# A decoder layer whose input is turned raw: root applied at read-out, merge gates scaled and put through tanh at the branch sums

## What is computed

```
h = x * rsqrt(mean(x^2) + 1e-6) * attn_norm
[MoBA q,k,v | NSA q, kv(cmp,slc,win) | NSA gates | merge gates] = h @ w_in
y_A = block-sparse attention (8 heads);  y_B = compressed, selected and window attention (8 heads, 2 kv groups)
x = x + (sigmoid(gA) * (y_A W_A) + sigmoid(gB) * (y_B W_B)) @ W_o
x = x + W_down(gelu(conv_a) * conv_b),  conv = causal conv3 of (RMSNorm(x) @ W_up)
x = x + sigmoid(x @ W_pg) * (p @ W_pp)
```

## Time and profile before

| | us |
|---|---|
| median of 3 runs | 888.48 |
| lowest, highest | 887.63, 891.33 |
| the profiled execution | 890.37 |
| its span, first to last instruction | 888.5 |
| busy PE, DVE, ACT, POOL | 863.6, 378.0, 405.8, 425.3 |

### The profile page before, as it was taken

How to read it: one execution, slowest core, us unless ns; L and a number is a source line. 1 busy time by engine, 2 the same in 40 slices (tenths; PEclk the granted TensorE clock), 3 DMA queues, 4 the chain that set the end, 5 groups by cost and what they waited for, 6 DMA issues and landing times.

```text
span 888.5 us, 13023 instructions
## 1 busy us (share of the span) xinstructions
PE 863.6 (97%) x4471; PEld 726.9 (82%) x4471; DVE 378.0 (43%) x864; ACT 405.8 (46%) x882; POOL 425.3 (48%) x547
## 2 busy tenths in 40 slices
PE   8999999999799999999999999999999999999998
PEld 8899889887688776788887888888888888888886
DVE  5446665555545534444417444444444440020223
ACT  5224656566646667533433744444444442231321
POOL 3841764554534345644552644444444444454440
PEclk9999999999999999999999999999999999999999
DMA  6944443342121226266531633333333333332214
GB/s 188 232 109 131 107 103 95 96 113 60 37 60 50 70 85 214 81 233 211 187 95 56 206 94 95 95 98 101 99 97 106 99 98 98 97 102 86 83 62 140
DMA packets 101363, 99.30 MB, mean 112 GB/s; under 512 B 15956, under 2 KB 76084, under 8 KB 101300
## 3 DMA queue, kind: packets, MB, share of 16 engines
q1 hardware_dynamic: 101247, 98.48, 37.7%
q10 hardware_dynamic: 53, 0.01, 0.0%
HBM read 87.58 MB, written 10.88 MB: 111 GB/s over the span
## 4 chain that ended last, share of the span: by engine, by line
PE 88%; DVE 4%; ACT 3%; issue 2%; POOL 2%; SPq 0%; DMA 0%; ACTq 0%; DVEq 0%; POOLq 0%
PE banks L1491 26%; PE banks L1492 25%; PE banks L1493 25%; PE banks L1672 3%; PE banks L1650 2%; PE banks L1630 1%; PE banks L1629 1%; PE banks L1551 1%; PE banks L1680 1%; ACT attention_split L875 1%; DVE plain_arena L1290 1%; DMA plain_arena<-in_conv_w_dram 0%; DVE plain_arena L1257 0%; PE banks L1579 0%; PE banks L1508 0%
## 5 line engine op out<-in xcount | busy, mean ns | idle before, releaser
L698 POOL TENSOR_TENSOR split_arena<-plain_arena,split_arena 128x512 fp32r<-128x512 f32 x184 | 240.2, 1318 | 252.0 <-ACT split_arena L932 232.5
L1491 PE MATMUL banks<-split_arena 128*128 128x512 f32 (+3 forms) x808 | 304.2, 376 | 5.3 <-ACT plain_arena L838 2.1
L1493 PE MATMUL banks<-split_arena 128*128 128x512 f32 (+3 forms) x808 | 296.8, 367 | 0.0
L1492 PE MATMUL banks<-split_arena 128*128 128x512 f32 (+3 forms) x808 | 296.7, 367 | 0.0
L932 ACT ACTIVATE split_arena<-plain_arena 128x512 fp32r<-128x512 f32 x184 | 112.9, 627 | 190.0 <-PE banks L1493 175.2
L1491 PEld LDWEIGHTS banks<-split_arena 128*128 128x128 f32 x808 | 152.4, 189 | 31.9 <-issue 3.5
L1493 PEld LDWEIGHTS banks<-split_arena 128*128 128x128 f32 x808 | 152.0, 188 | 21.1
L1492 PEld LDWEIGHTS banks<-split_arena 128*128 128x128 f32 x808 | 152.4, 189 | 20.3 <-issue 0.5
L1491 PE MATMUL banks<-late_arena,split_arena 128*128 128x512 f32 x240 | 93.8, 391 | 0.0
L1493 PE MATMUL banks<-late_arena,split_arena 128*128 128x512 f32 x240 | 93.5, 390 | 0.0
L1492 PE MATMUL banks<-late_arena,split_arena 128*128 128x512 f32 x240 | 93.5, 389 | 0.0
(11 more groups left out here) (193 smaller groups left out, 1113.4 us busy)
## 6 DMA issues: line engine op xcount, KB each, us to landing
plain_arena<-in_w_up_dram SPq DMA_DIRECT2D x88, 256.0 KB, 3.2
plain_arena<-in_w_down_dram SPq DMA_DIRECT2D x44, 256.0 KB, 2.6
plain_arena<-in_w_in_dram SPq DMA_DIRECT2D x18, 512.0 KB, 4.2
plain_arena<-in_w_in_dram SPq DMA_DIRECT2D x32, 192.0 KB, 4.0
plain_arena<-in_x_dram SPq DMA_DIRECT2D x8, 512.0 KB, 5.0
gates<-plain_arena SPq DMA_DIRECT2D x16, 256.0 KB, 2.4
plain_arena<-skew SPq DMA_DIRECT2D x16, 256.0 KB, 4.6
plain_arena<-gates SPq DMA_DIRECT2D x16, 256.0 KB, 3.6
```

Source lines behind the costliest of these rows:

```text
L698: pool.tensor_tensor(W2l[:, c % RING, :], raw2[:, c % RING, :], W2h[:, c % RING, :].bitcast(F32), ALU.subtract).then_inc(w2_lo, 1)
L1491: nc.tensor.matmul(o, ah, bh, start=first, stop=False)
L1492: nc.tensor.matmul(o, ah, bl, start=False, stop=False)
L1493: return nc.tensor.matmul(o, al, bh, start=False, stop=last)
```

## The change

x is turned as it comes, in two halves of 256 tokens; the squares and the root run beside it. `take_proj` multiplies each token tile by its root as it empties PSUM. Gates are kept and spilled raw; PE spreads the root over a 128 x 512 tile `rstd_row` (diagonal matrices times ones), and at the branch sums DVE multiplies each gate tile by it (`scale_gate_a`, `scale_gate_b`) and ACT applies the tanh (`tanh_gate_a`, `tanh_gate_b`). Gate b tiles get six places in memory (two used twice), and their loads move from chunks 15, 18 and 24 to 9, 13 and 15. Transfers are reordered: the gain first, x 0 and 1, the weights of unit 0, x 2 and 3, constants, then the rest. In unit 0 to 1, copies move from POOL to DVE, the high parts of unit 1 go to ACT and its low parts to DVE; POOL makes its table ahead of gate 0. In the steps, unit 3 is split one step earlier, unit 6 gets a second bank for one tile, and TILE and TURN of units 6 and 7 move (unit 6: TILE 35, 38, 39, 42, TURN 37, 40, 41, 44).

The diff, cut to its core (indentation of eight blanks taken off):

```diff
     row += count
-split0 = b0 - 8 if w == 7 else b0 - 7
+split0 = b0 - 8 if w in (3, 7) else b0 - 7
...
         late += 1
+    gap, lead = (3 if w == 6 else 2), (2 if w >= 6 else 1)
     for a in range(2):
-        TILE[t + 2 + late + 2 * a], TURN[t + 3 + late + 2 * a] = (w, 2 * half + a), (w, 2 * half + a)
+        TILE[t + 2 + late + gap * a], TURN[t + 2 + late + gap * a + lead] = (w, 2 * half + a), (w, 2 * half + a)
...
         eng.wait_ge(raw0_in[kt // 4], 32)
-        eng.wait_ge(x_sq, NT)
...
         return 7 * (tt % 2)
+    if w == 6:
+        return 7 * (tt == 1)
...
 def vec_bank(w, x):
-    return 4 if w <= 1 and x % 2 else 1
+    if w == 0:
+        return (1, 4, 3, 5)[x]
+    return 4 if w == 1 and x % 2 else 1
...
+def turned_part(half, kt):
...
+    wk = A["w_in"].rearrange("l (k p) n -> p (l k) n", p=P)
+    sp.dma_start(rows[0:8, 0, :], A["attn_norm"].rearrange("l (r c) -> (l r) c", c=P)).then_inc(gain_in, 16)
+    for half in range(2):
+        for tt in range(2 * half, 2 * half + 2):
+            sp.dma_start(xnat[:, tt, :], x_d[tt]).then_inc(x_in[tt], 16)
+        if half == 0:
+            for part in range(2):
+                ks = slice(4 * part, 4 * part + 4)
+                sp.dma_start(raw[:, ks, 0:256], wk[:, ks, C_KC:C_KC + 256]).then_inc(raw0_in[part], 16)
+                sp.dma_start(raw[:, ks, 256:280], wk[:, ks, C_NG:C_NG + 24]).then_inc(raw0_in[part], 16)
...
         sp.dma_start(w2c[:, v, :], A[nm].rearrange("l k n -> (l k) n")).then_inc(w2c_in, 16)
-    sp.wait_ge(x_turned, KT)
-    sp.dma_start(w1[0], w1_d[0]).then_inc(w1k_in, 16)
...
     sp.dma_start(w1[1], w1_d[1]).then_inc(w1k_in, 16)
+    sp.wait_ge(x_turned, 2 * KT)
+    sp.wait_ge(x_sq, NT)
+    sp.dma_start(w1[0], w1_d[0]).then_inc(w1k_in, 16)
...
     def load_gate_b(k):
-        if k >= 2:
-            sp.wait_ge(br_sum, k - 1)
-        sp.dma_start(gb[:, k % 2, :], gate_d[8 + k]).then_inc(gb_in[k % 2], 16)
+        if k >= 6:
+            sp.wait_ge(br_sum, k - 5)
+        elif k >= 2:
+            sp.wait_ge(pv_done, values_count[T - 1])
+        if k >= 4:
+            sp.wait_ge(gb_scaled, k // 2 * 2 - 2)
...
         load_chunk(c)
-        if c == 15:
+        if c == 9:
...
             load_gate_b(3)
+        if c == 13:
+            load_gate_b(4)
+            load_gate_b(5)
+        if c == 15:
+            load_gate_b(6)
+            load_gate_b(7)
...
             load_gates_a(1)
-            load_gate_b(4)
-            load_gate_b(5)
...
-        if c == 24:
-            load_gate_b(6)
-            load_gate_b(7)
...
-    split_gate(0)
...
     ins.then_inc(rtab_done, 1)
-    pool.wait_ge(cst_done, 1)
-    for tt in range(2):
-        pool.wait_ge(qkv_done, tt + 1)
-        for a in range(2):
-            ins = pool.tensor_copy(qn[:, tt, :, a * DH:(a + 1) * DH], qkv[:, tt, 0:256].rearrange("p (v c) -> p v c", v=4))
-    ins.then_inc(dup_pool, 1)
-    split_unit(1, range(KT))
+    split_gate(0)
+    pool.wait_ge(cst_done, 2)
...
             act.wait_ge(g_out, 16 * j)
-        nc.scalar.activation(gstage, PS[:, 7, :], ACT.Tanh, scale=0.5).then_inc(gate_tanh, 1)
+        nc.scalar.activation(gstage, PS[:, 7, :], ACT.Copy).then_inc(gate_taken, 1)
...
+    def h_high(half, kt):
+        act.wait_ge(x_turned, KT * half + kt // 2 * 2 + 2)
+        nc.scalar.activation(hTh[:, kt, 256 * half:256 * half + 256], turned_part(half, kt), ACT.Copy, scale=cst[:, kt:kt + 1]).then_inc(hT_hi, 1)
...
+    act.wait_ge(cst_turned, 1)
+    nc.scalar.activation(cst[:, 0:8], PS[:, 0, 0:8], ACT.Copy).then_inc(cst_done, 1)
+    square_x(0)
     act.wait_ge(cst_done, 1)
+    for kt in range(4):
+        h_high(0, kt)
+    for k in (0, 2):
+        w_high(0, range(k, k + 2))
+        h_high(0, k + 4)
+        h_high(0, k + 5)
+    w_high(0, range(4, KT))
+    square_x(2)
     for kt in range(KT):
-        act.wait_ge(x_turned, kt + 1)
-        nc.scalar.activation(hTh[:, kt, :], PS[:, turn_bank(kt), :], ACT.Copy, scale=cst[:, kt:kt + 1]).then_inc(hT_hi, 1)
+        h_high(1, kt)
+    w_high(1, range(KT))
+    act.wait_ge(cst_turned, 4)
+    nc.scalar.activation(cst[:, 8:CONVW + P + 4], PS[:, 2, 8:CONVW + P + 4], ACT.Copy).then_inc(cst_done, 1)
...
     nc.scalar.activation(gsig, qkv[:, :, 256:280], ACT.Tanh, scale=0.5).then_inc(gsig_tanh, 1)
+    act.wait_ge(rstd_spread, 1)
+    nc.scalar.activation(rstd_row, PS[:, 6, :], ACT.Copy).then_inc(rstd_row_done, 1)
...
+    def tanh_gate_a(i):
+        act.wait_ge(ga_scaled, i + 1)
+        nc.scalar.activation(ga[:, i % 4, :], ga[:, i % 4, :], ACT.Tanh, scale=0.5).then_inc(ga_tanh, 1)
...
+    def tanh_gate_b(i):
+        act.wait_ge(gb_scaled, i + 1)
+        nc.scalar.activation(gb[i], gb[i], ACT.Tanh, scale=0.5).then_inc(gb_tanh, 1)
...
+    for i in range(4):
+        tanh_gate_a(i)
...
         e = c - RING
+        if e == 2:
+            for i in range(4):
+                tanh_gate_b(i)
+        if e == 8:
+            tanh_gate_b(4)
+            tanh_gate_b(5)
+        if e == 12:
+            for i in range(4, 8):
+                tanh_gate_a(i)
+        if e == 13:
+            tanh_gate_b(6)
+            tanh_gate_b(7)
...
+    def square_x(tt):
+        dve.wait_ge(x_in[tt], 16)
+        nc.vector.tensor_tensor_reduce(out=square_out[:, tt, :], in0=xnat[:, tt, :], in1=xnat[:, tt, :], scale=1.0, scalar=0.0,
+                                       op0=ALU.mult, op1=ALU.add, accum_out=ssx[:, tt:tt + 1]).then_inc(x_sq, 1)
...
+    def h_low(half):
+        for kt in range(KT):
+            q = slice(256 * half, 256 * half + 256)
+            dve.wait_ge(hT_hi, KT * half + kt // 2 * 2 + 2)
+            nc.vector.scalar_tensor_tensor(out=hTl[:, kt, q], in0=turned_part(half, kt), scalar=cst[:, kt:kt + 1],
+                                           in1=hTh[:, kt, q].bitcast(F32), op0=ALU.mult, op1=ALU.subtract).then_inc(hT_lo, 1)
...
+    square_x(1)
+    dve.wait_ge(cst_done, 1)
+    h_low(0)
+    square_x(3)
+    h_low(1)
+    gate_high(0)
+    gate_low(0)
     dve.wait_ge(x_sq, NT)
+    rsqrt(rstd, ssx, 1.0 / D, 4)
     dve.wait_ge(pool_const, 4)
+    for tt in range(NT):
+        ins = nc.vector.tensor_scalar(rstd_diag[:, tt * P:(tt + 1) * P], ident, rstd[:, tt:tt + 1], None, ALU.mult)
+        if tt == 0:
+            ins.then_inc(rstd_done, 1)
+    ins.then_inc(rdiag_done, 1)
+    for tt in range(2):
+        dve.wait_ge(qkv_done, tt + 1)
+        for a in range(2):
+            ins = nc.vector.tensor_copy(qn[:, tt, :, a * DH:(a + 1) * DH], qkv[:, tt, 0:256].rearrange("p (v c) -> p v c", v=4))
+    ins.then_inc(dup_dve, 1)
...
+    def shift_tokens(x):
+        dve.wait_ge(tcmp_a, x + 1)
+        nc.vector.tensor_copy(tcmp[DH:P, x, 0:S - 1], PS[DH:P, vec_bank(0, x), 1:S]).then_inc(tcmp_b, 1)
...
+    for kt in range(4):
+        w_low_one(1, kt)
+    for x in range(2):
+        shift_tokens(x)
+    for kt in range(4, KT):
+        w_low_one(1, kt)
+    for x in range(2, 4):
+        shift_tokens(x)
+    dve.wait_ge(cst_done, 2)
...
         link(nc.vector.tensor_scalar(cst[:, c:c + 1], cst[:, c:c + 1], -(DH ** -0.5), None, ALU.mult))
-    gate_high(0)
-    gate_low(0)
-    split_unit(1, range(KT))
...
+    def scale_gate_a(i):
+        dve.wait_ge(ga_in, 64 * (i // 4 + 1))
+        nc.vector.tensor_tensor(ga[:, i % 4, :], ga[:, i % 4, :], rstd_row, ALU.mult).then_inc(ga_scaled, 1)
...
+    def scale_gate_b(i):
+        dve.wait_ge(gb_in[i // 2 % 2], 32 * (i // 4 + 1))
+        nc.vector.tensor_tensor(gb[i], gb[i], rstd_row, ALU.mult).then_inc(gb_scaled, 1)
...
+    dve.wait_ge(rstd_row_done, 1)
...
         for m in range(4):
+            scale_gate_a(4 * mg + m)
+        for m in range(4):
             dve.wait_ge(chunk_done, cidx[("bra", mg, 3)] + 1)
-            dve.wait_ge(ga_in[m], 16 * (mg + 1))
+            dve.wait_ge(ga_tanh, 4 * mg + m + 1)
...
                                            op0=ALU.add, op1=ALU.mult).then_inc(brA_done, 1)
+        for i in range(4) if mg == 0 else (6, 7):
+            scale_gate_b(i)
...
             dve.wait_ge(chunk_done, cidx[("brb", mg, 3)] + 1)
-            dve.wait_ge(gb_in[i % 2], 16 * (i // 2 + 1))
+            dve.wait_ge(gb_tanh, i + 1)
             dve.wait_ge(brA_done, i + 1)
-            nc.vector.scalar_tensor_tensor(out=gb[:, i % 2, :], in0=gb[:, i % 2, :], scalar=1.0, in1=PS[:, 4 + m, :],
+            nc.vector.scalar_tensor_tensor(out=gb[i], in0=gb[i], scalar=1.0, in1=PS[:, 4 + m, :],
...
             dve.wait_ge(brB_done, i + 1)
-            nc.vector.tensor_tensor(ga[:, m, :], ga[:, m, :], gb[:, i % 2, :], ALU.add).then_inc(br_sum, 1)
+            nc.vector.tensor_tensor(ga[:, m, :], ga[:, m, :], gb[i], ALU.add).then_inc(br_sum, 1)
...
                                            op0=ALU.mult, op1=ALU.subtract).then_inc(mT_lo, 1)
+        if mg == 0:
+            scale_gate_b(4)
+            scale_gate_b(5)
...
     def turn_consts():
-        pe.wait_ge(const_in, 16 * 11)
+        pe.wait_ge(const_in, 16 * 10)
```

(37 more changed lines are left out.)

137 lines of the change are left out of this document (59 added, 78 removed).

## The result

The changed kernel takes 896.66 us (median of 4 runs, 895.23 to 897.89) where the kernel before takes 888.06 beside it: a ratio of 1.0086, 95% interval 1.0068 to 1.0104. It is slower, by 8.6 us; the forecast was 8.1 us faster. Its profiled execution took 897.32 us, with a span of 895.5 against 888.5.

The account below looks back on a forecast made before the run. PE, busy 863.6 of 888.5 us, was taken as the bound, so only its stands and slow-clock stretches could pay. Gains of 13.5 less losses of 5.4 gave net -8.1, a median of 880.4 us, range 872 to 886.

Parts of the forecast that it names:

- Opening: Kernel start to compression: turning x raw starts the first product near 9.6 us and saves 6.5 us (bounds 4 and 8).
- PE does not starve: Unit 0's products: POOL delivers a weight slice each 0.75 us and PE needs one each 0.77, so no waits.
- Unit 3's split: Attention steps: splitting one step earlier removes most of 1.9 us of PE waits for low halves, -1.5 us.
- Unit 6's bank: Attention steps: a second bank removes PE's 1.3 us wait for the previous take-out, -1.2 us.
- Unit 6's turns: Tile transposes: normalising two steps ahead removes 5.0 us of waits, leaves some 1.5, -3.0 us; slow clock behind them, -1.3.
- Unit 7's wider lead: Attention steps, unit 7: normalisation further ahead of the transposes; left without a price, entered as nothing.
- Branch sums: First brb chunk of group 1: take_x, queued behind ACT's tanh, makes PE wait, +4.4 us, and +1.0 for the clock.
- strict lock: Branch sums: each of two scalings might wait for a whole POOL operation, some 2 us more, 882.4; not used in the sum.
- (4): Attention steps: their own latency takes back all 7.0 us of gains while the branch wait stays, 887.4; chance 0.06.
- Rival (1): Branch sums: the wait is hidden, b gates load early and take_x is in time, 875; chance 0.22.
- Rival (2): Kernel start gains only 2.5 us, PE cold or POOL late: 884.5, or 885.5 if turn waits stay; chance 0.17.
- Rival (3): Branch sums: waits through the b gates close a loop, PE starves at chunks 12 to 20, slower, 894; chance 0.05.

Follow-up runs that it names:

- experiment 5: Changed kernel with the old step for the split of unit 3: 895.36 us, ratio 1.0068.
- experiment 4: Changed kernel with unit 6's old steps: 895.28 us; kernel with tanh moved, old split, unit 7 as before, unit 6's transposes evenly at 37, 39, 41, 43: 882.12 us.
- experiment 2: Changed kernel with GpSimd's low halves of weight chunks 10 to 19 cut to one column of 512: 888.75 us, ratio 0.9994.
- the plan alone: Kernel before with only unit 3's earlier split, unit 6's second bank and the later transposes of units 6 and 7: 892.89 us, ratio 1.0038.
- turn7_half1: Changed kernel with the old lead of one step for unit 7's first two transposes only: 893.37 us, ratio 1.0042.

## Why the prediction was wrong

It forecast a span 8.1 us shorter; it was 7.0 longer. The 15.1 us come apart by its own terms: unit 6's turns and clock 4.3, the branch sums 3.1, unit 7 3.0, unit 3's split 2.3, the opening 1.7, the bank 0.3, and 0.4 open. So no single step explains the miss; the largest are named first here and taken in the order of the kernel below.

- **Opening, -6.5 forecast, -4.8 measured** (25.69 for 31.32, and 0.8 of the +1.6 behind it; the other 0.8 is the split). Compression itself starts 5.0 us sooner. The mechanism held in the main: no stand at the transposes, the position adds as the new latest thing. Sizes were off. The 12 warm-ups last 4.98 us and I had let them end in time for the gains; ACT's first high halves ended at 9.57 for 8.3, and the first product came at 10.86 for 9.6. "PE does not starve" was wrong by 0.58 us (15.52 above): seven of POOL's eight slices kept the pace of 0.75 us, but the one beside DVE's square of a tile (1.57 us from 13.26) took 1.76. The 0.8 us for the clock was not needed in this form: behind the first product PEclk read 1.00. The adds ended at 47.57 and PE began compression at 47.67, where 45.8 to 46.1 was forecast. The terms given for POOL's chain there (37.4, 0.7, 1.8, 5.6) sum to 45.5 and not 46.1, so that the adds would be latest did not follow from them.
- **Unit 3's split, -1.5 forecast, +0.8 measured.** This is a step that failed, not a size: I took the wait from the earlier trace rows away and did not ask what comes later if the split comes sooner. The root and the normalisation did, and PE waited 1.49 us at the transposes (and 1.23 at later ones) for the 1.7 us of split waits removed (experiment 5).
- **Unit 6's bank, -1.2 forecast, -0.9 measured.** Right.
- **Unit 6's turns, -3.0, and clock, -1.3, forecast; 0.0 measured.** The prediction named the wait for the shared bank at step 41 and gave it 1.5 us; it was 2.57, just as long as the one it replaced, and the slow stretch behind such a wait came with it. At full clock the steps are worth 1.0 (experiment 4). The failed term is the size of that wait, and the clock term was hung on it.
- **Unit 7's wider lead, "nothing that rows let me price"; +3.0 measured.** The failed step. The trace of the kernel before did allow a bound: DVE's low halves of a turned tile, 1.1 us, and their wait for ACT would land in a step where GpSimd's 3.3 us of root already stood ahead of what PE wants, and where PE waited 0.9 us already. A move without a price was entered as zero.
- **Branch sums, +5.4 forecast, +8.5 measured.** Place, chain and name of the late instruction were right, to the first brb chunk of group 1. The wait grew by 6.0 where 4.4 was taken, and the clock cost 2.6 where 1.0 was. The term that was mis-sized is the duration of DVE's work beside GpSimd, and in the part of the chain that I had not charged with it: the low halves took 1.44 us each on average for the 0.90 of the earlier trace rows, because three of the four ran beside GpSimd and not one (experiment 2). The sentence that took the ports as a strict lock added 2 us to the wait, for 6.8 in all; 6.4 was measured, but it had put the lock at the two scalings, which met no GpSimd work.
- **0.4 us** between values 1 and 3 are open. They are not in the plan alone (63.07 there, 63.12 before, 63.5 in all kernels with the new opening and raw gates). No run isolates them.

Of the rivals, (4), attention gains taken back while the branch wait stays, comes nearest to what happened; it had a chance of 0.06, and it let the steps go back to zero where they went to +3. Rival (1), no wait for take_x, came true in no run with this order on ACT: 2.15 us of wait stayed even with most of GpSimd's work gone. Rival (2), an opening that gains 2.5, did not come either; its second figure was a slip, since with the turn waits back 884.5 goes to at least 887.5 and not 885.5. Rival (3), the loop through the b gates, would have starved PE at chunks 12 to 20: behind the 6.4 us wait PE stood only once more in the whole changed kernel, for 0.5 us, and with only the tanh moved, the loads and their waits on SP unchanged, the loss is gone. The range erred because the four priced terms in attention were all gains taken from waits seen in rows, the fifth was entered as zero, and none had a chance to be negative.

## What to carry to other kernels

In a plan written out by hand, price a moved step by what the receiving step holds on every engine, not by the wait that it removes: three of the four moves here brought new waits that took back most of the gain or more than all of it. An instruction that waits for a slow chain and is not needed soon goes behind everything in its queue that PE does need soon; two lines moved gave 8.8 us. And where DVE works on two SBUF inputs beside GpSimd, take the duration of each instruction that meets the other's, one by one (1.77 us here), not the average of a group of which some were alone.

## What the runs showed of the hardware

- DVE instructions of two SBUF inputs, 128 x 512 f32: 0.68 us each alone, one every 0.60, and 1.77 us each, one every 1.70, beside GpSimd's instructions of the same form. GpSimd's take 1.74 us there and 1.29 without DVE's. From 406.8 us on in the changed kernel the two alternate: four of DVE's in 6.41 us, four of GpSimd's in 6.32.
- A wait of 2.6 us was followed by a stretch at a granted 0.5 in nine of eleven profiled executions, and cost 1.4 to 2.6 us each time. The 6.2 to 6.8 us waits were followed by it every time, in five. The same kernel can go either way: turn7_half1 took 890.32 us in its profiled execution, without a slow stretch at unit 6 (mean granted clock 0.996), and 893.00 to 894.83 in its nine others (0.991 to 0.994), of which there is no trace but whose mean clock tells of more slow time. So a clock term behind a wait of 2.6 us is a matter of chance from run to run, and two kernels are best compared stretch by stretch at the same granted clock.
- At the start of the kernel the PEclk column reads 1.00 while PE runs at up to twice the usual duration: the first 24 warm-up records take 4.98 us, 0.21 each, the sixteen from 8.39 us 1.95 in all, 0.12 each; in the kernel with 6 warm-ups the first 12 take 2.93 us, 0.24 each. There a stretch of the opening shows 8 transposes in 1.75 us at a reading of 1.00 (PE, PEld, DVE, ACT, POOL, PEclk, DMA share, GB/s):

```profile
5.00:7.00 2.00, 1.75 (x8) 1.75 (x9) 0.48 (x1) 1.53 (x4) 0.00 (x0) 1.00 0.99 342
```

The durations fit the 1.2 GHz at which, by the Trainium skill ("TensorE: Matmul & The Clock Gate", section "What's actually happening"), the engine stands while cold; the column does not show it. Fewer warm-ups moved the slow time onto the transposes. The moment of the rise differed between executions: the same 24 records took 4.28 to 5.49 us, and with them the end of unit 0 moved from 24.1 to 26.4, more than the edit to the warm-ups did.
